# A third value group as seven block products, the rotary table built early, and the log decays stored at once

## The chip, the cores and the metric

The kernel runs on one core of a Trainium2 chip. The metric is the device time of one execution in microseconds (us), lower is better. The kernel before took 2183.36 us (median of three runs, 2181.09 to 2188.8).

## The reference, cut to what matters

One layer of a streaming encoder on a sequence of 1024 tokens with 1024 channels, in float32. The change touches the combined projection and what follows from it directly:

```python
h = rmsnorm(x, ln_pre_mix)
p = h @ w_in
(g_q, g_k, g_v, g_r, g_lr, r_q, r_k, r_v, r_g, a_gla, a_ret) = split(p)
log_a = log_sigmoid(g_lr @ w_gla_decay + b_gla_decay) / GLA_TAU   # log decays of the GLA branch
o_gla = gla_mixer(g_q, g_k, g_v, log_a)                           # gated linear attention, chunks of 64
rq, rk = rope(r_q, positions), rope(r_k, positions)               # cos and sin of positions * inv_freq
o_ret = retention_mixer(rq, rk, r_v)
...
```

Behind it come the output projections of both branches, a mixing projection, and a convolutional feed-forward layer. The change leaves these alone.

## The kernel before

**Numbers and products.** Every float32 matmul is made of three single-pass ones (`product3`, L475 to L477): both operands are split into a high part and a rest (`w_hi`, `w_lo`, `act_hi`, `act_lo`), and high x high, high x rest and rest x high are added up in PSUM. ScalarE or GpSimd makes the high parts, GpSimd or VectorE the rests.

**Queues.** The order of the work on each engine is written out by hand, one function for each engine and stage, with semaphores between them. SyncE's queue (SP) issues nearly all DMAs. SP is in order: behind an instruction that waits, every later DMA waits too.

**The projection stage** runs in this order on TensorE (`proj_pe`):

1. value groups 0 and 1, "plain": each takes 512 columns of values, 8 token tiles by 8 parts of the contraction, so 192 matmuls of 512 columns in two halves of 96;
2. 44 rows of the projection in 22 pairs (`rows_pe`), each pair as seven block products (Strassen's scheme in Winograd's form) of 12 matmuls of 512 columns. The seven use sums of blocks of the activations, `a_sums`, which VectorE and ScalarE make beside value groups 0 and 1 (`rows_sums`, `block_hi`). The last of the seven needs the fourth sum, `S4`;
3. value groups as seven block products (`block_values_pe`), each product 48 matmuls of 256 columns. There are `BLOCK_GROUPS = 2` of them;
4. the small product for the decays' low-rank input (`small_product`, L705 and L706), 32 matmuls;
5. the rest of the value groups, plain. There are six groups in all, so two are left: `EARLY_GROUPS` (call it A) and `EARLY_GROUPS + 1` (B). In the first half of A, `decay_inputs` puts in two times four small matmuls (L718) that give the decays' logits.

**What runs beside A and B.** VectorE and ScalarE turn the logits into log decays (`log_a`, L760 to L805). Then VectorE computes the rotary table in `ang`, `turn` and `rope_out` (a range reduction of 11 steps, L810 to L826, two steps behind the sines), ScalarE takes two sines (L767, L768). GpSimd splits the slabs of B and the first slabs of the next stage (L509, L512). SP stores the values of A, then loads slabs, stores `log_a` (2 MB), stores the table (1 MB), stores more values, waits for both tables to land, and issues the first loads of the next stage (`gla_first_loads`): masks, interval table, two chunks of log decays, keys, queries and values of two tiles, and the gates. The values of B are stored last, and `proj_sp` ends when these stores have landed.

**The GLA stage** begins on TensorE in `first_tile`: `decay(0, 0)` needs the split log decays of the first tile, two pieces of a side projection follow, then `scores(0, 0)`, `decay(0, 1)`, two more pieces, `scores(0, 1)`. ScalarE's order there is `decay(0)`, an eviction, `log_a_hi(2)` (the split of the next chunk of log decays), `decay(1)`. VectorE's `queries(0, 1)` and so `scores(0, 1)` need `decay(1)`. The loads that `log_a_hi(2)` needs are the first DMAs that SP issues in its next phase (`gla_sp`), thus after the last value stores have landed:

```python
            for j in range(RING):
                sp.wait_ge(stored[j], 16 * PROJ_STORES)
```

Of the kernel before, what the change touches and what calls it, by code (L numbers as in the profile page):

```python
# [21 lines left out]
I32 = mybir.dt.int32  # L22
# [8 lines left out]
P = 128  # L31
# [64 lines left out]
RING = 4  # L96
SL_VAL = 0
SL_LR = SL_VAL + 4 * EARLY_GROUPS
BLOCK_GROUPS = 2
# [141 lines left out]
def build(nc, x, positions, w_stream, w_dec, b_dec, ln_post_mix, ln_post_ffn, ln_cols_in, conv_in,  # L241
          ident_in, interval_in, masks_in, ret_dec_in, ret_q_in, ret_k_in, inv_freq_in, eps_in, out):
    ctx = ExitStack()
    with ctx:
# [24 lines left out]
        stat = sb(ctx, "stat", (P, 80))  # L269
        with ExitStack() as s:  # L270
            act_f = [sb(s, f"act_f{i}", (P, KT * SEQ)) for i in range(2)]
# [14 lines left out]
        with ExitStack() as s:  # L286
# [8 lines left out]
            pos_i = sb(s, "pos_i", (P, SEQ), I32)  # L295
            ang = sb(s, "ang", (P, 2, SEQ))
            turn = sb(s, "turn", (P, SEQ))
            rope_out = sb(s, "rope_out", (P, 2, SEQ))
            invf = sb(s, "invf", (P, 1))
# [88 lines left out]
        row_s1 = at(88, "row_s1", (P, 2, HALF))  # L388

# [127 lines left out]
        def norm_sp(sp):  # L517
# [11 lines left out]
            load_slab(sp, 3, 3)  # L529

# [107 lines left out]
        def proj_pe(pe):  # L638
# [82 lines left out]
        def proj_act(act):  # L721
# [44 lines left out]
            act.wait_ge(sem["angle"], ANGLE_STEPS - 2)  # L766
            nc.scalar.activation(rope_out[:, 1, :], ang[:, 0, :], ACT.Sin).then_inc(sem["sin_half"], 1)  # L767
            nc.scalar.activation(ang[:, 1, :], ang[:, 0, :], ACT.Sin, scale=0.5).then_inc(sem["sin_half"], 1)  # L768

            values(EARLY_GROUPS, range(2, 4))  # L770
            values(EARLY_GROUPS + 1, range(2))
            gla_first_parts(act)
            values(EARLY_GROUPS + 1, range(2, 4))

        def proj_dve(dve):
# [25 lines left out]
            for t in range(NT):  # L801
                if t >= 2:
# [7 lines left out]
            nc.vector.tensor_copy(ang[:, 1, :], pos_i[:, :]).then_inc(sem["angle"], 1)  # L810
            dve.wait_ge(sem["angle"], 1)
            nc.vector.tensor_scalar(ang[:, 0, :], ang[:, 1, :], invf[:, 0:1], None, ALU.mult
                                    ).then_inc(sem["angle"], 1)
            dve.wait_ge(sem["angle"], 2)
            magic = 1.5 * 2.0 ** 23
            nc.vector.tensor_scalar(turn[:, :], ang[:, 0, :], 1.0 / (2.0 * math.pi), magic,
                                    ALU.mult, ALU.add).then_inc(sem["angle"], 1)
            dve.wait_ge(sem["angle"], 3)
            nc.vector.tensor_scalar(turn[:, :], turn[:, :], magic, None, ALU.subtract
                                    ).then_inc(sem["angle"], 1)  # L820
            dve.wait_ge(sem["angle"], 4)
            for i, part in enumerate(two_pi_parts()):
                nc.vector.scalar_tensor_tensor(ang[:, 0, :], turn[:, :], -part, ang[:, 0, :],
                                               ALU.mult, ALU.add).then_inc(sem["angle"], 1)
                dve.wait_ge(sem["angle"], i + 5)
            nc.vector.tensor_scalar(ang[:, 0, :], ang[:, 0, :], 3.1415925, -3.1415925,  # L826
                                    ALU.min, ALU.max).then_inc(sem["angle"], 1)
            dve.wait_ge(sem["sin_half"], 2)
            nc.vector.tensor_tensor(ang[:, 0, :], ang[:, 1, :], ang[:, 1, :], ALU.mult
                                    ).then_inc(sem["angle"], 1)  # L830
            dve.wait_ge(sem["angle"], ANGLE_STEPS - 1)
            nc.vector.tensor_scalar(rope_out[:, 0, :], ang[:, 0, :], -2.0, 1.0, ALU.mult, ALU.add
                                    ).then_inc(sem["angle"], 1)

        def proj_sp(sp):
# [17 lines left out]
            value_stores(1, range(4))  # L853
# [31 lines left out]
            block_store(sp, 1, 1)  # L885
            block_store(sp, 1, 0)
            sp.wait_ge(sem["lr_out"], 1)
# [3 lines left out]
            sp.dma_start(pos_i[:, :], positions.to_broadcast((P, SEQ))).then_inc(sem["small_in"], 16)  # L891
            sp.dma_start(invf[:, :], inv_freq_in).then_inc(sem["small_in"], 16)
            for n in range(SL_LR + RING, SL_LR + 2 * RING + 1):
                load(n)
            for g in range(EARLY_GROUPS, N_PLAIN):
                value_stores(g, range(2))
                for n in range(4 * g + 2 * RING + 1, 4 * g + 3 * RING + 1):
                    if n < SL_SIDE + 7:
                        load(n)
                if g == EARLY_GROUPS:  # L900
                    sp.wait_ge(sem["log_a"], NT)
                    sp.dma_start(loga_d.rearrange("t p c -> p t c"), z_sb[:, :, :]).then_inc(sem["tables_stored"], 16)
                    sp.wait_ge(sem["angle"], ANGLE_STEPS)
                    sp.dma_start(rope_d.rearrange("a p n -> p a n"), rope_out[:, :, :]
                                 ).then_inc(sem["tables_stored"], 16)
                value_stores(g, range(2, 4))
                if g == EARLY_GROUPS:
                    sp.wait_ge(sem["tables_stored"], 32)
                    for j in range(RING):
                        sp.wait_ge(stored[j], 16 * (EARLY_GROUPS + ROW_LOADS))  # L910
# [3296 lines left out]
```

## Time and profile before

| what | value |
|---|---|
| median of three runs | 2183.36 us |
| the profiled execution | 2180.39 us |
| its span, first to last instruction | 2178.2 us |
| TensorE busy | 2140.4 us, 98% of the span |
| VectorE, GpSimd, ScalarE busy | 61%, 61%, 36% |
| mean granted TensorE clock | 0.998 |
| mean DMA rate | 144 GB/s |

Matmuls are pipelined, so the time from the start of one to the start of the next tells more than their durations; a stage's length is the difference between two starts. Idle time of an engine other than TensorE costs something only where TensorE waits for it in the end.

### The profile page before, as it was taken

How to read it: one execution, taken by the hardware profiler on the slowest of the kernel's cores; microseconds unless marked ns; L12 is line 12 of the kernel's file. 1: busy time of each engine (PE TensorE's matmuls, PEld its weight loads, DVE VectorE, ACT ScalarE, POOL GpSimd, SP SyncE). 2: the span in 40 equal slices, each digit the busy share in tenths (PEclk: the TensorE clock that was granted, in tenths of full speed). 3: DMA queues.
4: the chain of work that ended last, by engine and by line, in shares of the span. 5: the costliest groups of instructions: out<-in, count | busy, mean ns of one | idle time of the engine just before them, and what ended most of it. 6: DMA issues, size and time to landing. Idle time of an engine off the chain costs nothing. (4 is left out here: it accounts for less than half of the span.)

```text
span 2178.2 us, 28844 instructions
## 1 busy us (share of the span) xinstructions
PE 2140.4 (98%) x10682; PEld 1762.2 (81%) x10682; DVE 1323.6 (61%) x1702; ACT 781.1 (36%) x1275; POOL 1321.8 (61%) x907
## 2 busy tenths in 40 slices
PE   8999999999999999999999999999999999999998
PEld 7888888888988788887776888878778888887887
DVE  7422222222263777768778159854877777779988
ACT  4323333322122222222224134545444444444445
POOL 4787777776554666569875412520799999972000
PEclk9999999999999999999999999999999999999999
DMA  4233333332337344356666755973122332247463
GB/s 178 85 118 107 116 116 117 116 101 94 111 120 247 98 140 141 121 184 179 183 176 212 270 179 150 252 202 133 61 78 88 87 88 87 78 163 251 155 228 134
DMA packets 212729, 312.85 MB, mean 144 GB/s; under 512 B 12464, under 2 KB 129584, under 8 KB 212592
## 3 DMA queue, kind: packets, MB, share of 16 engines
q1 hardware_dynamic: 210272, 306.76, 43.7%
q0 software_dynamic: 2176, 4.19, 1.2%
q8 instruction: 86, 1.41, 0.3%
q14 instruction: 51, 0.42, 0.1%
q10 hardware_dynamic: 144, 0.07, 0.0%
HBM read 220.79 MB, written 90.18 MB: 143 GB/s over the span
## 5 line engine op out<-in xcount | busy, mean ns | idle before, releaser
L475 PE MATMUL psum<-act_hi,w_hi 128*128 128x512 f32 x976 | 389.1, 399 | 3.3 <-POOL w_lo L3802 1.2
L477 PE MATMUL psum<-act_hi,w_lo 128*128 128x512 f32 x976 | 381.0, 390 | 0.0
L476 PE MATMUL psum<-act_lo,w_hi 128*128 128x512 f32 x976 | 380.7, 390 | 0.0
L475 PEld LDWEIGHTS psum<-act_hi,w_hi 128*128 128x128 f32 x976 | 183.3, 188 | 42.9 <-POOL w_lo L3802 2.5
L477 PEld LDWEIGHTS psum<-act_hi,w_lo 128*128 128x128 f32 x976 | 183.2, 188 | 39.5
L475 PE MATMUL psum<-w_hi 128*128 128x512 f32 x532 | 208.4, 392 | 6.3 <-DVE w_lo L3433 5.1
L476 PEld LDWEIGHTS psum<-act_lo,w_hi 128*128 128x128 f32 x976 | 183.5, 188 | 35.7
L477 PE MATMUL psum<-w_hi,w_lo 128*128 128x512 f32 x532 | 207.7, 390 | 0.0
L476 PE MATMUL psum<-w_lo,w_hi 128*128 128x512 f32 x532 | 207.6, 390 | 0.0
L1117 POOL TENSOR_TENSOR w_lo<-w_raw,w_hi 128x512 fp32r<-128x512 f32 x88 | 115.3, 1311 | 70.7 <-ACT w_hi L1075 70.7
L475 PE MATMUL psum<-w_hi,act_hi 128*128 128x512 f32 (+1 forms) x384 | 139.7, 364 | 1.7 <-POOL w_lo L512 1.5
L476 PE MATMUL psum<-w_lo,act_hi 128*128 128x512 f32 (+1 forms) x384 | 139.3, 363 | 0.0
L477 PE MATMUL psum<-w_hi,act_lo 128*128 128x512 f32 (+1 forms) x384 | 139.2, 363 | 0.0
L475 PE MATMUL psum<-a_sums,w_hi 128*128 128x512 f32 x352 | 136.9, 389 | 0.0
L476 PE MATMUL psum<-a_sums,w_hi 128*128 128x512 f32 x352 | 136.9, 389 | 0.0
L477 PE MATMUL psum<-a_sums,w_lo 128*128 128x512 f32 x352 | 136.9, 389 | 0.0
L3802 POOL TENSOR_TENSOR w_lo<-w_raw,w_hi 128x512 fp32r<-128x512 f32 x80 | 125.5, 1578 | 2.8 <-ACT w_hi L3863 2.8
L475 PEld LDWEIGHTS psum<-w_hi 128*128 128x128 f32 x532 | 100.2, 188 | 30.2 <-POOL w_lo L3439 5.0
L477 PEld LDWEIGHTS psum<-w_hi,w_lo 128*128 128x128 f32 x532 | 100.2, 188 | 21.1
L476 PEld LDWEIGHTS psum<-w_lo,w_hi 128*128 128x128 f32 x532 | 100.3, 189 | 20.5
L1117 POOL TENSOR_TENSOR w_lo<-t_sums,w_hi 128x512 fp32r<-128x512 f32 x66 | 85.0, 1289 | 43.3 <-ACT w_hi L1075 43.3
L3863 ACT ACTIVATE w_hi<-u_t 128x512 fp32r<-128x512 f32 x66 | 39.8, 628 | 194.0 <-POOL u_t L3788 120.3
(392 smaller groups left out, 5219.3 us busy)
## 6 DMA issues: line engine op xcount, KB each, us to landing
w_raw<-in_w_stream SPq DMA_DIRECT2D x161, 512.0 KB, 4.3
proj_scratch<-stage SPq DMA_DIRECT2D x44, 512.0 KB, 5.2
r_x<-proj_scratch SPq DMA_DIRECT2D x64, 256.0 KB, 3.7
w_raw<-ffn_scratch SPq DMA_DIRECT2D x55, 256.0 KB, 3.1
value_scratch<-stage SPq DMA_DIRECT2D x24, 512.0 KB, 3.6
w_raw<-in_w_stream SPq DMA_DIRECT2D x44, 256.0 KB, 4.9
ffn_scratch<-u_lin_v SPq DMA_DIRECT2D x22, 512.0 KB, 5.9
w_raw<-ffn_scratch SPq DMA_DIRECT2D x22, 512.0 KB, 4.3
```

The lines of the kernel that those rows point to most:

```text
L475: nc.tensor.matmul(o, s_hi, m_hi, start=start, stop=False)
L476: nc.tensor.matmul(o, s_hi, m_lo, start=False, stop=False)
L477: return nc.tensor.matmul(o, s_lo, m_hi, start=False, stop=stop)
L1117: nc.gpsimd.tensor_tensor(w_lo8[:, n % 8, :], row_block(p, i), w_hi8[:, n % 8, :].bitcast(F32), ALU.subtract).then_inc(sem["u_lo"], 1)
L3802: nc.gpsimd.tensor_tensor(w_lo8[:, n % 8, :], block_raw(p, i), w_hi8[:, n % 8, :].bitcast(F32), ALU.subtract).then_inc(sem["u_lo"], 1)
L3863: nc.scalar.activation(w_hi8[:, n % 8, :], block_raw(p, i), ACT.Copy).then_inc(sem["u_hi"], 1)
```

## The change

One of the two late plain value groups (B) becomes a third block group, so the stage ends with A alone. The rotary table is computed beside value groups 0 and 1, between the sums of activation blocks, in memory that the fourth sum and `row_s1` use later: ScalarE therefore waits for the stored table before it writes the fourth sum's high part. The log decays are stored right behind the first half of A's values. The masks and the interval table are loaded before the wait for the stores, and the loads of the next stage's slabs 4 to 6 stand between and behind the other first loads. The positions and inverse frequencies are loaded at the very start and no longer in front of the decays.

```diff
-BLOCK_GROUPS = 2
+BLOCK_GROUPS = 3
...
@@ norm_sp
             load_slab(sp, 3, 3)
+            sp.dma_start(pos_i[:, :], positions.to_broadcast((P, SEQ))).then_inc(sem["small_in"], 16)
+            sp.dma_start(invf[:, :], inv_freq_in).then_inc(sem["small_in"], 16)
@@ proj_pe
-            for a in range(2):
-                pe.wait_ge(sem["val_evac"], 4 * EARLY_GROUPS + 2 + 2 * a)
-                values(EARLY_GROUPS + 1, a)
@@ proj_act
-            block_hi(8, S4R_HI, S4_F)
             for n in range(6):
                 row_hi(act, n)
+            act.wait_ge(sem["angle"], ANGLE_STEPS - 2)
+            nc.scalar.activation(sines[:, :], ang[:, :], ACT.Sin).then_inc(sem["sin_half"], 1)
+            nc.scalar.activation(turn[:, :], ang[:, :], ACT.Sin, scale=0.5).then_inc(sem["sin_half"], 1)
             values(1, range(2, 4))
             row_hi(act, 6)
             row_hi(act, 7)
+            act.wait_ge(sem["tables_stored"], 32)
+            block_hi(8, S4R_HI, S4_F)
             rows_act(act)
...
             values(EARLY_GROUPS, range(2))
-            act.wait_ge(sem["angle"], ANGLE_STEPS - 2)
-            nc.scalar.activation(rope_out[:, 1, :], ang[:, 0, :], ACT.Sin).then_inc(sem["sin_half"], 1)
-            nc.scalar.activation(ang[:, 1, :], ang[:, 0, :], ACT.Sin, scale=0.5).then_inc(sem["sin_half"], 1)
-
+            gla_first_parts(act)
             values(EARLY_GROUPS, range(2, 4))
-            values(EARLY_GROUPS + 1, range(2))
-            gla_first_parts(act)
-            values(EARLY_GROUPS + 1, range(2, 4))
@@ proj_sp
             value_stores(0, range(2, 4))
-            value_stores(1, range(4))
+            value_stores(1, range(2))
+            sp.wait_ge(sem["angle"], ANGLE_STEPS)
+            sp.wait_ge(sem["sin_half"], 1)
+            sp.dma_start(rope_d[0, :, :], ang[:, :]).then_inc(sem["tables_stored"], 16)
+            sp.dma_start(rope_d[1, :, :], sines[:, :]).then_inc(sem["tables_stored"], 16)
+            value_stores(1, range(2, 4))
...
+            value_stores(EARLY_GROUPS, range(2))
+            sp.wait_ge(sem["log_a"], NT)
+            sp.dma_start(loga_d.rearrange("t p c -> p t c"), z_sb[:, :, :]).then_inc(sem["tables_stored"], 16)
+            gla_table_loads(sp)
+            sp.wait_ge(sem["tables_stored"], 48)
+            for j in range(RING):
+                sp.wait_ge(stored[j], 16 * (EARLY_GROUPS + ROW_LOADS))
+            gla_log_a_load(sp, 0)
+            gla_log_a_load(sp, 1)
+            load(SL_SIDE + 4)
+            gla_first_loads(sp)
+            load(SL_SIDE + 5)
+            load(SL_SIDE + 6)
+            value_stores(EARLY_GROUPS, range(2, 4))
@@ rows_sums (VectorE)
             lo(2, S2_LO, S2_F, S2_HI)
+            angle_turns(dve)
+            angle_reduce(dve, 0, 3)
             lo(3, S3_LO, S3_F, S3_HI)
+            angle_reduce(dve, 3, 7)
+            nc.vector.tensor_scalar(ang[:, :], ang[:, :], 3.1415925, -3.1415925, ALU.min, ALU.max
+                                    ).then_inc(sem["angle"], 1)
+            angle_cosines(dve)
             lo(4, S4_LO, S4_F, S4R_HI)
```

`angle_turns`, `angle_reduce` and `angle_cosines` hold the same steps as L810 to L832 before: four, seven, and the two behind the sines. `gla_table_loads` is the masks' and the interval table's load, taken out of `gla_first_loads`.

## Rows read from the trace of the kernel before

**Rows 1.** The page: busy time of each engine.

```profile
PE 2140.4 (98%) x10682; PEld 1762.2 (81%) x10682; DVE 1323.6 (61%) x1702; ACT 781.1 (36%) x1275; POOL 1321.8 (61%) x907
```

**Rows 2.** Waits of TensorE, whole span: total us, times, longest.

```profile
PE psum L718 <- DVE lr_parts L789: 0.9, 1, 0.9
PE psum L475 <- ACT stage L731: 0.9, 1, 0.9
```

**Rows 3.** Windows: first block group, group B. Busy by engine, clock, DMA share, GB/s.

```profile
524.48:564.80 40.32, 40.32 (x338) 40.31 (x337) 7.95 (x7) 8.33 (x8) 26.20 (x11) 1.00 0.27 96
...
658.90:702.40 43.50, 43.50 (x193) 35.88 (x192) 14.21 (x7) 8.14 (x9) 21.44 (x9) 1.00 0.79 260
```

**Rows 4.** Timeline of TensorE: start us, duration us, then the operation.

```profile
618.89 1.20 PE L718 MATMUL psum<-wd_parts,lr_parts 128*128 128x512 f32 x4 [0.89 <-DVE lr_parts L789]
...
625.40 1.07 PE L718 MATMUL psum<-wd_parts,lr_parts 128*128 128x512 f32 x4
...
702.90 0.47 PE L1855 MATMUL psum<-interval,la_parts 128*128 128x512 f32 x1 [0.27 <-issue]
```

**Rows 5.** Timeline of ScalarE, from the decays' input to the second decay.

```profile
616.77 0.63 ACT L751 ACTIVATE wd_parts<-wd_raw 128x512 fp32r<-128x512 f32 x1 [33.36 <-DMA invf<-in_inv_freq_in]
...
639.96 1.92 ACT L731 ACTIVATE stage<-psum 128x1024 f32<-128x1024 f32 x2
...
711.54 0.63 ACT L1525 ACTIVATE la_parts<-g_la 128x512 fp32r<-128x512 f32 x1 [0.51 <-DMA g_la<-loga_scratch]
712.35 1.14 ACT L1561 ACTIVATE e_t<-psum 128x1152 f32<-128x1152 f32 x1 [0.18 <-PE psum L1859]
```

**Rows 6.** Timeline of SP: start us, then the time until the last of the group was issued.

```profile
610.43 0.42 SPq L890 DMA_DIRECT2D b_all<-in_b_dec  x1
...
703.72 1.29 SPq L839 DMA_DIRECT2D value_scratch<-stage  x2
708.41 1.09 SPq L1460 DMA_DIRECT2D g_la<-loga_scratch  x2
```

**Rows 7.** DMA issues of four stretches (from 607, 666, 681, 700 us): us from issue to landing.

```profile
b_all<-in_b_dec SPq DMA_DIRECT2D x1, 256.0 KB, 3.5
...
loga_scratch<-z_sb SPq DMA_DIRECT2D x1, 2048.0 KB, 9.4
...
g_gate<-proj_scratch SPq DMA_DIRECT2D x1, 512.0 KB, 7.1
value_scratch<-stage SPq DMA_DIRECT2D x1, 512.0 KB, 7.9
...
value_scratch<-stage SPq DMA_DIRECT2D x2, 512.0 KB, 3.4
g_la<-loga_scratch SPq DMA_DIRECT2D x2, 128.0 KB, 2.6
```

**Rows 8.** Windows: the first loads' long part, and the end of them.

```profile
684.00:693.00 9.00, 9.00 (x42) 7.44 (x41) 3.49 (x2) 2.36 (x3) 5.75 (x3) 1.00 1.11 289
693.00:700.00 7.00, 7.00 (x33) 5.79 (x32) 0.00 (x0) 0.00 (x0) 5.76 (x4) 1.00 0.97 359
```

**Rows 9.** Timeline of VectorE: the last log decay and the range reduction.

```profile
640.08 0.69 DVE L798 SCALAR_TENSOR_TENSOR z_sb<-z_sb,z_a 128x512 f32<-128x512 f32 x1 [0.64 <-ACT z_a L763]
...
643.66 21.31 DVE L823 SCALAR_TENSOR_TENSOR ang<-turn,ang 128x1024 f32<-128x1024 f32 x7
```

**Rows 10.** Timelines beside value group 1 and the first rows: VectorE, ScalarE, TensorE.

```profile
87.82 4.49 DVE L1008 TENSOR_TENSOR a_sums<-a_sums_f,a_sums 128x2048 fp32r<-128x2048 f32 x2 [7.21 <-ACT a_sums L735]
...
105.80 1.94 ACT L731 ACTIVATE stage<-psum 128x1024 f32<-128x1024 f32 x2 [4.23 <-PE psum L477]
...
121.92 0.39 PE L475 MATMUL psum<-a_sums,w_hi 128*128 128x512 f32 x1
```

**Rows 11.** Windows near the end of the span, where TensorE waits often.

```profile
1975.00:1980.00 5.00, 2.88 (x12) 2.05 (x11) 5.00 (x4) 2.10 (x4) 5.00 (x4) 0.97 0.14 36
1980.00:1990.00 10.00, 10.00 (x39) 8.13 (x38) 9.86 (x9) 1.79 (x3) 2.62 (x2) 0.85 0.79 255
```

More of the change, by code:

```diff
@@ L269, in build @@
         stat = sb(ctx, "stat", (P, 80))
+        invf = sb(ctx, "invf", (P, 1))
         with ExitStack() as s:
@@ L388, in build @@
         row_s1 = at(88, "row_s1", (P, 2, HALF))
+        turn, ang = at(72, "turn", (P, SEQ)), at(76, "ang", (P, SEQ))
+        pos_i, sines = at(88, "pos_i", (P, SEQ), I32), at(88, "sines", (P, SEQ))
         u_cg = [at(0, "u_cg0", (P, SEQ)), at(4, "u_cg1", (P, SEQ))]
@@ L808, in proj_dve @@
             log_a_tail(NT - 1)
[L810 to L833, printed above, removed]
         def proj_sp(sp):
@@ L890, in proj_sp @@
             sp.dma_start(b_all[:, :], b_dec.to_broadcast((P, GLA_QK))).then_inc(sem["small_in"], 16)
-            sp.dma_start(pos_i[:, :], positions.to_broadcast((P, SEQ))).then_inc(sem["small_in"], 16)
-            sp.dma_start(invf[:, :], inv_freq_in).then_inc(sem["small_in"], 16)
             for n in range(SL_LR + RING, SL_LR + 2 * RING + 1):
                 load(n)
[L895 to L910, printed above, removed]
-                    gla_first_loads(sp)
+            value_stores(EARLY_GROUPS, range(2))
[12 more added lines that the diff above has]
+            value_stores(EARLY_GROUPS, range(2, 4))
             for j in range(RING):
@@ L998, in build, with angle_turns, angle_reduce, angle_cosines @@
         S1_F, S4_F, S2_F, S3_F = [a_sums_f[i] for i in (0, 2, 3, 1)]
+        def angle_turns(dve):
+            dve.wait_ge(sem["small_in"], 32)
+            nc.vector.tensor_copy(ang[:, :], pos_i[:, :]).then_inc(sem["angle"], 1)
+            dve.wait_ge(sem["angle"], 1)
+            nc.vector.tensor_scalar(ang[:, :], ang[:, :], invf[:, 0:1], None, ALU.mult).then_inc(sem["angle"], 1)
+            dve.wait_ge(sem["angle"], 2)
+            magic = 1.5 * 2.0 ** 23
+            nc.vector.tensor_scalar(turn[:, :], ang[:, :], 1.0 / (2.0 * math.pi), magic,
+                                    ALU.mult, ALU.add).then_inc(sem["angle"], 1)
+            dve.wait_ge(sem["angle"], 3)
+            nc.vector.tensor_scalar(turn[:, :], turn[:, :], magic, None, ALU.subtract).then_inc(sem["angle"], 1)
+            dve.wait_ge(sem["angle"], 4)
+        def angle_reduce(dve, lo, hi):
+            for i in range(lo, hi):
+                nc.vector.scalar_tensor_tensor(ang[:, :], turn[:, :], -two_pi_parts()[i], ang[:, :],
+                                               ALU.mult, ALU.add).then_inc(sem["angle"], 1)
+                dve.wait_ge(sem["angle"], i + 5)
+        def angle_cosines(dve):
+            dve.wait_ge(sem["sin_half"], 2)
+            nc.vector.tensor_tensor(ang[:, :], turn[:, :], turn[:, :], ALU.mult).then_inc(sem["angle"], 1)
+            dve.wait_ge(sem["angle"], ANGLE_STEPS - 1)
+            nc.vector.tensor_scalar(ang[:, :], ang[:, :], -2.0, 1.0, ALU.mult, ALU.add).then_inc(sem["angle"], 1)
         def rows_sums(dve):
```

14 lines of the change are left out of this document (6 added, 8 removed).

## The prediction

> **What bounds the kernel now.** I read the page first. TensorE is busy for 98% of the span, and the three other compute engines for 61% or less [rows 1]. So time changes only where TensorE gets fewer or shorter matmuls, or where it waits. Then I read TensorE's waits over the whole span. In the stretch that the change touches they hold two entries of 0.9 us: one for the split input of the decays (L718 behind VectorE's `lr_parts`), one for the last eviction of group B (L475 behind ScalarE's L731) [rows 2]. The reader is to see that no wait of this stretch is large: a gain must come from matmuls, and a loss from waits that aren't there yet. Third, windows give the lengths of the pieces: a block group takes 40.32 us, plain group B 43.5 us, at a full clock, and in the block group the weight loads fill the whole window (40.31 us) [rows 3]. Last come the timelines of the engines and of SP from 600 to 715 us, since group B is also the cover under which the log decays are stored, read back and split, and the first tiles are loaded.
>
> **Term 1: the group.** Plain B is 192 matmuls of 512 columns, 43.5 / 192 = 227 ns each. A block group is 7 x 48 = 336 matmuls of 256 columns, 40.32 / 336 = 120 ns each [rows 3]. The multiplications fall by an eighth (168 against 192 in units of 512 columns), but a 256-column matmul costs more than half of a 512-column one, so the gain is 43.5 - 40.3 = 3.2 us. VectorE (8 us of 40), ScalarE (8) and GpSimd (26) have room in such a window [rows 3], so I expect the third group to run at the pace of the first.
>
> A rule of the Trainium skill speaks of this price: in "TensorE: Matmul & The Clock Gate", section "Back-to-back issue gap", a warm matmul takes N / 2.4 + 2.5 ns, thus 109 ns for 256 columns and 216 ns for 512. By it the term would be 41.4 - 36.7 = 4.7 us instead of 3.2. The rows above show 120 and 227 ns, and weight loads without a gap, so the measurement decides.
>
> **Term 2: the decays' input.** ScalarE's L751 started at 616.77 us, when the load of `invf` had landed [rows 5]. That load and the positions now come at the start of the kernel. The last load in front of L751 is then `b_all`, issued at 610.43 to 610.85 and landed 3.5 us later, at 614.4 [rows 6, 7]. L751 comes 2.4 us earlier relative to the small product, which is more than the 0.9 us that TensorE waits [rows 2, 4]. Gain 0.9 us.
>
> **Term 3: the table beside groups 0 and 1.** Here I must price what the front now has to wait for. VectorE gets 14 more operations of 128x1024 ahead of the fourth sum. A two-input operation of twice that size takes 4.49 / 2 = 2.24 us there, so about 1.1 us each. Beside a busy GpSimd the seven reduction steps took 21.31 / 7 = 3.04 us each [rows 9, 10]. Before, VectorE ended its sums at 87.82 + 4.49 = 92.3 us. It stood idle for 7.2 us before them; four short steps (0.7 us each, an estimate) and three reductions at 1.1 fit in there. Behind the third sum (90.1 us) come four reductions and the clamp: 5.3 us cheap, 15.2 us dear. They end between 95 and 105 us. The sines need ScalarE (about 1.3 us of table load and twice 1.05 us): 102 (it is held by TensorE's pace until then) to 108 us. The cosines add 2 to 4 us, the two stores 3.4 us [rows 7], so the table has landed between 109 and 116 us. Then ScalarE's part of the fourth sum takes 1.9 us, VectorE's 2.24 to 4.4 us: ready between 113 and 122 us. TensorE uses it at 121.92 us [rows 10]. GpSimd is idle or paced by TensorE for half of that time, so I take the cheap side, with 5 us to spare: cost 0. Dear end: 1 us. The evictions of group 1 (L731 at 105.80 us [rows 10]) slip by at most 3 us, and TensorE needs their banks only at the fifth row product, 11 us later. Queued behind ScalarE's new wait are `row_s1` and the high parts of the second pair, needed eight products (22 us) after 105.6 us: covered. At the very start SP issues two more DMAs behind the first slabs: covered too.
>
> **Term 4: what lay under group B.** Everything up to the small product moves by 40.3 us, and the decays' chain by 40.3 - 0.9 = 39.4 us. The GLA stage would start at 702.90 - 3.2 - 0.9 = 698.8 us, if its inputs are there. Now the chain:
>
> - The last log decay was ready at 640.08 + 0.69 = 640.8 us, the first half of A's values evicted at 641.9 us [rows 5, 9]. After: 680.2 and 681.3 us.
> - SP issues both value stores and then the 2 MB store at 681.7 us. It took 9.4 us before [rows 7]. Half a slab's load lay ahead of it then and the table's store (1 MB) came behind it; I take 8.5 us, thus 690.2 us, and 691.1 as the late end, 688.5 as the early one.
> - Four DMAs read two chunks back (2.2 us to issue, 2.6 us to land [rows 6, 7]): 695.0 us. ScalarE and VectorE split the second chunk in 0.6 + 0.7 to 2.9 us (the upper end is what a VectorE operation took beside GpSimd): 696.3 to 698.5 us. TensorE wants it at 698.8 us. No cost, barely; at the late end 0.6 us.
> - All the first loads are now behind that wait. From 691 us on, SP has to move the two chunks (0.5 MB), a slab (0.5), five loads of keys, values and gates (2.6), two slabs (1.05) and the last two value stores (1.05), 5.8 MB in all. The stretch in which such loads ran moved 289 GB/s, the one behind it 359 [rows 8]: 1.05 / 0.359 + 2.6 / 0.289 + 2.1 / 0.359 = 2.9 + 9.0 + 5.8 = 17.7 us. The last store has landed at about 709 us. It can't be earlier than 700.9 + 3.4 = 704.3 us, the issue plus the landing without a backlog [rows 7]; with the 7.9 us of a store behind the gates [rows 7] and two slabs more (2.9 us) it is 711.7 us.
> - Before, the last stores were issued at 703.72 us, `proj_sp` ended with their landing, and `gla_sp` issued the next log decays at 708.41 us. ScalarE was already waiting for them at 711.54 us, and `decay(1)` ran at 712.35 us [rows 5, 6]. ScalarE is in order, so `decay(1)`, VectorE's `queries(0, 1)` and TensorE's `scores(0, 1)` stand behind that load. With SP free at about 709.4 us, `decay(1)` runs 1.0 us later than before. Without this wait it would have run 4.1 us earlier.
>
> So the stall in front of `scores(0, 1)` is about 5 us, and it takes up any shorter wait before it (late `g_la`, late keys for `queries(0, 0)`); they don't add.
>
> **Sum.** -3.2 - 0.9 + 5.1 = +1.0 us on the profiled execution's 2180.39 us (span 2178.2 and 2.2 around it). The median of the runs is 2183.36 us, 3.0 us above; the same change there gives **2184.4 us**. From the bounds: -4.1 with the early end of the stores, +3.3 with the late one, +1 more from the front and +1.5 from the clock (below).
>
> **Rivals.**
>
> 1. *The backlog drains in time* (0.27). The DMAs of the first tiles land fast enough that the last store lands at about 704.3 us. For it: DMA moved 359 GB/s where nothing slow was in the way. Against it: 5.8 MB between 691 and 704 would need 440 GB/s. Part of the way is possible: between -4.1 and -1 us, 2179.3 to 2182.4 us.
> 2. *The log decays come back late, and the clock falls* (0.10). The one mechanism is the 2 MB store: each us that it lands later delays first tile and last store alike. From 5.5 us more than I take (14 us instead of 8.5) the loss passes 6.5 us, 2190 us or more. Near the end of the span, where TensorE worked 2.88 of 5 us, the granted clock went from 1.00 to 0.85 over 10 us, that is, to 1.2 GHz for a part of it [rows 11], which costs 1.5 us. A stall of 5 us or more could do that here. The Trainium skill, "TensorE: Matmul & The Clock Gate", section "What's actually happening", has the same rule: the clock is halved when the engine was idle. By it rival 2 and my forecast would be up to 1.5 us longer.
> 3. *The front binds* (0.05). The fourth sum comes behind 121.92 us because the reduction runs at 3.04 us a step throughout: +1 to +4 us on top, 2185 to 2189 us.
> 4. *The group is cheaper than the row says* (0.03), at the page's 109 ns per matmul: the third group and the two others would have to differ. 336 x 0.011 = 3.7 us more, 2181 us.
> 5. Something that I don't see, either way (0.03). My own case has 0.52.
>
> **Numbers.** About 0.3% (6.5 us) is what a measurement of this kernel can tell from no change. Nearly all cases lie within it; the ends count through the scatter of runs (2181 to 2189 us). Faster 0.11, same 0.76, slower 0.13. The range reaches from the drained backlog less 1.3 us of scatter to rival 2's beginning: 2178 to 2190 us.
>
> **What would show it.** Right: three windows of 40.3 us for the block groups; no wait at L718; the table's stores landed before 116 us and no TensorE wait near 122 us; GLA's first L1855 at about 699 us; a wait of some 5 us of TensorE in front of the second L1873 group; ScalarE's L1525 for the third chunk waiting on DMA `g_la`; SP's first L1460 of the next phase at about 709 us. Wrong: if that L1460 is at 704 to 705 us, rival 1 holds; if L1855 itself starts behind 702 us, the store of the log decays was later than I took; if the clock falls under 1.00 at 710 us, its cost is on top.

## The result, and the profile after

The changed kernel took 2195.2 us (median of 18 runs, 2184.49 to 2200.82), the kernel before 2183.83 us beside it (18 runs, 2179.55 to 2189.14). The ratio is 1.0047 with an interval of 1.0035 to 1.0058: slower, by 0.5%, more than the scatter of the runs explains, and 5 us beyond the end of my range. The profiled execution of the changed kernel took 2194.13 us (span 2192.3).

TensorE's waits over the whole span of the changed kernel (total us, times, longest), to be read against [rows 2]:

```profile
PE psum L1882 <- DVE k_lev L1734: 7.5, 3, 6.0
...
PE psum L473 <- POOL w_lo L2576: 5.0, 2, 4.1
...
PE psum L715 <- DVE lr_parts L784: 1.8, 1, 1.8
```

The first is the stall in front of `scores(0, 1)` that Term 4 describes. The second is in the y stage, 600 us later, where the diff changes nothing. The third is the split input of the decays, 0.9 us in [rows 2].

Windows of the three block groups, of the first tile, and of the y stage (us; busy time of TensorE, its weight loads, VectorE, ScalarE, GpSimd; clock; DMA share; GB/s):

```profile
524.90:565.30 40.40, 40.40 (x339) 40.40 (x338) 8.02 (x8) 8.39 (x9) 26.22 (x11) 1.00 0.27 93
565.30:605.60 40.30, 40.30 (x338) 40.30 (x337) 8.46 (x8) 8.31 (x9) 26.26 (x11) 1.00 0.32 106
605.60:645.60 40.00, 40.00 (x336) 40.00 (x334) 8.43 (x7) 5.11 (x5) 14.40 (x12) 1.00 0.30 106
...
709.00:716.00 7.00, 6.99 (x48) 5.53 (x44) 1.02 (x3) 0.19 (x1) 0.00 (x0) 1.00 0.55 204
716.00:724.00 8.00, 2.03 (x31) 1.92 (x31) 4.42 (x7) 2.77 (x4) 4.19 (x4) 0.66 0.40 125
718.51:721.97 3.46, 0.00 (x1) 0.00 (x1) 2.57 (x5) 1.35 (x2) 2.14 (x2) 0.50 0.20 48
721.97:725.34 3.37, 3.37 (x35) 3.06 (x36) 2.67 (x5) 0.63 (x1) 3.29 (x4) 0.50 0.33 106
...
1330.00:1340.00 10.00, 5.88 (x26) 4.59 (x25) 7.96 (x12) 4.96 (x8) 10.00 (x2) 0.99 0.56 158
```

The third group runs at the pace of the first. From 716 us on TensorE has 2.03 us of work in 8, and the granted clock falls to 0.50 (1.2 GHz) for 6.8 us, from 718.51 to 725.34 us. The wait lasts until 721.97 us, so half of this stretch lies in the wait and costs nothing. In the other half, 3.4 us, TensorE works at half speed: that costs 1.7 us on top of the wait.

SP from the log decays' store to the third chunk's load (start us, us until issued), to be read against [rows 6]:

```profile
682.68 1.29 SPq L809 DMA_DIRECT2D value_scratch<-stage  x2
684.02 0.49 SPq L874 DMA_DIRECT2D loga_scratch<-z_sb  x1
...
693.84 1.15 SPq L1468 DMA_DIRECT2D g_la<-loga_scratch  x2
...
698.55 2.58 SPq L1455 DMA_DIRECT2D g_v<-value_scratch  x1
701.17 0.47 SPq L1448 DMA_DIRECT2D g_gate<-proj_scratch  x1
701.69 2.67 SPq L489 DMA_DIRECT2D w_raw<-in_w_stream  x2
704.40 0.94 SPq L809 DMA_DIRECT2D value_scratch<-stage  x2
714.52 1.09 SPq L1468 DMA_DIRECT2D g_la<-loga_scratch  x2
```

ScalarE and TensorE behind it, against [rows 5] and [rows 4]:

```profile
656.36 0.63 ACT L752 ACTIVATE wd_parts<-wd_raw 128x512 fp32r<-128x512 f32 x1 [32.46 <-DMA b_all<-in_b_dec]
...
717.72 0.63 ACT L1534 ACTIVATE la_parts<-g_la 128x512 fp32r<-128x512 f32 x1 [8.53 <-DMA g_la<-loga_scratch]
718.26 1.11 ACT L1570 ACTIVATE e_t<-psum 128x1152 f32<-128x1152 f32 x1
```

```profile
701.18 0.47 PE L1864 MATMUL psum<-interval,la_parts 128*128 128x512 f32 x1 [0.38 <-DVE la_parts L1670]
...
721.97 1.55 PE L1882 MATMUL psum<-q_lev,k_lev 128*64 128x64 f32 x24 [5.98 <-DVE k_lev L1734]
```

The reader should see one chain: the last value stores are issued at 704.40 us, the next load waits for their landing until 714.52 us, ScalarE waits 8.53 us for that load, `decay(1)` runs at 718.26 us instead of 712.35, and TensorE stands 5.98 us.

DMA landings of the stretch 700 to 706 us, against [rows 7]. The last value stores took 8.6 us to land behind the gates and the slabs, 3.4 us before:

```profile
w_raw<-in_w_stream SPq DMA_DIRECT2D x2, 512.0 KB, 7.3
value_scratch<-stage SPq DMA_DIRECT2D x2, 512.0 KB, 8.6
```

### Where the time lies, in many traces

One trace was not enough here. The table sets the start of the same TensorE matmul in a run against its start in the first trace of the kernel before (us later; the columns are times in that trace). The column 60 stands ahead of all work that the edits move, apart from two small loads.

```
trace                 60    740    921   1300   1345   1500    end
before, 2nd        -0.2   -0.1   -0.5    2.0    2.0    4.7    4.7
before, 3rd         2.0    2.1    2.0    1.6    1.6    4.6    4.8
changed, 1st        0.2    5.7    5.9    7.4   13.5   13.9   14.0
changed, 2nd        0.1    6.0    5.6    7.0    7.0    7.7    7.7
changed, 3rd        0.6    6.1    6.0    5.4   11.3   16.0   16.1
changed, 4th        2.2    8.2    7.8    9.1    9.1   14.9   15.2
group_only          0.0   24.3   24.6   23.7   23.7   26.3   26.5
table_early         0.1   -0.8    0.8    3.0    3.0    2.7    2.6
stores_first        1.6    5.8    5.0    4.4    4.4   10.1   10.2
keep_busy           0.1    4.2    3.1    4.4    7.2   13.8   13.9
backlog_more        0.2    8.0    7.2    6.6    6.6    5.7    5.9
bias_apart          1.7    4.8    4.9    4.5    4.5    7.4    7.4
chunks_first        2.0   -2.5   -3.2   -2.2   -2.2   -1.6   -1.4
before_shift        1.9    7.7    6.8    5.7    5.7   10.1    9.9
after_y             0.2    7.6    7.6    8.8   16.6   19.3   19.4
after_y19           2.1    8.1    7.4    8.9    8.9   12.3   12.3
chunks_y19          2.0   -2.5   -2.8   -1.7   -1.7    0.7    0.8
before_y            1.8    2.0    1.9    4.1    4.1    2.6    2.7
chunks_y            0.4   -4.0   -4.3   -4.8   -4.8   -2.4   -2.4
```

Four places move. The start of the kernel, ahead of 60 us, differs by up to 2.4 us from execution to execution, in both kernels (mean 0.8 and 0.6): the traces that are 1.6 us or more late at 60 us have 3.4 us of half clock near 15 us, the others none. To read the effect of an edit on the first tile, take the column 60 off. The first tile is in every trace of the changed kernel: 5.5 to 6.0 us with the start taken off (mean 5.7) against 0.0 to 0.1 in the kernel before. The y stage (1300 to 1345) costs 6 us in two of the four and nothing in the others: in the first trace 4.1 us of a wait, and 1.7 us for the half clock behind it. The mix stage (1469 us) costs 0 to 3 us in the kernel before and 0.4 to 5.8 in the changed one (mean 1.9 and 2.9). So 0.1 + 5.7 + 3.0 + 1.0 and 0.2 in between make 10 us of the medians' 11.4.

### The profile page after: what moved, and what is told of

It reads as the page before. It is cut to its first block and busy times, and to the rows that moved or that the text cites. A ratio compares the mean times of both kernels' runs of the same rounds, so it can differ in the third digit from the quotient of the medians.

```text
span 2192.3 us, 29169 instructions
## 1 busy us (share of the span) xinstructions
PE 2142.1 (98%) x10826; PEld 1768.6 (81%) x10826; DVE 1323.8 (60%) x1709; ACT 786.0 (36%) x1279; POOL 1335.2 (61%) x910
## 3 DMA queue, kind: packets, MB, share of 16 engines
q0 software_dynamic: 2176, 4.19, 1.2%
## 5 line engine op out<-in xcount | busy, mean ns | idle before, releaser
L473 PE MATMUL psum<-w_hi,act_hi 128*128 128x512 f32 (+1 forms) x368 | 128.4, 349 | 1.9 <-POOL w_lo L510 1.6
L474 PE MATMUL psum<-w_lo,act_hi 128*128 128x512 f32 (+1 forms) x368 | 127.9, 348 | 0.0
L475 PE MATMUL psum<-w_hi,act_lo 128*128 128x512 f32 (+1 forms) x368 | 127.9, 348 | 0.0
L1125 POOL TENSOR_TENSOR w_lo<-t_sums,w_hi 128x512 fp32r<-128x512 f32 x66 | 87.3, 1323 | 39.4 <-ACT w_hi L1083 39.4
```

Of the source, the lines that this page charges most:

```text
L473: nc.tensor.matmul(o, s_hi, m_hi, start=start, stop=False)
L474: nc.tensor.matmul(o, s_hi, m_lo, start=False, stop=False)
L475: return nc.tensor.matmul(o, s_lo, m_hi, start=False, stop=stop)
L1125: nc.gpsimd.tensor_tensor(w_lo8[:, n % 8, :], row_block(p, i), w_hi8[:, n % 8, :].bitcast(F32), ALU.subtract).then_inc(sem["u_lo"], 1)
```

## The experiments

**group_only and table_early**: the two halves of the change, each alone.

```diff
 group_only: the kernel before with
-BLOCK_GROUPS = 2
+BLOCK_GROUPS = 3
-            for a in range(2):
-                values(EARLY_GROUPS + 1, a)
 table_early: the changed kernel with BLOCK_GROUPS = 2 and group B plain and last
```

> Only the third block group: the rotary table stays behind the log decays, and the stores and loads of the stage's end stay in their old order, now under group A alone. Nothing is left out. Late-store theory: the 2 MB store waits behind the loads of slabs that follow GpSimd's pace (about 705 us instead of 684), then come 9 us of store and 3 us of loads, so the GLA stage begins near 722 us instead of 701, and the time is 15 to 25 us above the kernel before. If the cover of the stores did not matter, it would be 3 us below.

> Only the early rotary table and the early store of the log decays, with two block groups and group B plain again. Nothing is left out. Late-store theory: group B covers the stores and first loads again, so there is no long wait in the first tile; within 2 us of the kernel before, 0 to 1 us better if the wait at the decays' input shrinks. Rival (the front costs something that the trace of one execution doesn't show, such as slower sums of activation blocks): 3 us or more above the kernel before, with a TensorE wait near 122 us. Rival (the y stage suffers from any shift of the stages before it): a wait in the y stage here too.

group_only: 2206.73 us, 23.7 over the kernel before, and one wait of TensorE of 24.5 us at the GLA stage's first matmul, with a half clock of 23.9 us. That is inside the forecast. table_early: 2185.47 us, ratio 1.0014 (1.0004 to 1.0024), and no wait of 1 us in the first tile. The median is 2.4 us over the kernel before, a little more than the 2 us that I allowed for. The third group brings the loss with it, since it takes away the cover of group B: under a plain group B the last stores land in time. The early table and the early store of the log decays bring that loss down, from 24 us to 11.

**stores_first**: are the loads ahead of the last value stores what costs?

```diff
             gla_log_a_load(sp, 1)
-            load(SL_SIDE + 4)
-            gla_first_loads(sp)
-            load(SL_SIDE + 5)
-            load(SL_SIDE + 6)
+            gla_tile_loads(sp, 0)
             value_stores(EARLY_GROUPS, range(2, 4))
+            gla_log_a_load(sp, 2)
...
 def gla_sp
+            gla_tile_loads(sp, 1)
+            gla_gates(sp, 0)
+            for n in range(SL_SIDE + 4, SL_SIDE + 7):
+                stream_load(sp, n)
             for t in range(NT):
```

> The changed kernel, with the late half of A's value stores issued right behind the first tile's loads, the third chunk of log decays loaded behind them while SP is still in the projection stage, and the second tile's loads, the gates and slabs 4 to 6 moved behind the end of proj_sp. Nothing is left out of the computation. Late-store theory (the loss is the wait for the landing of the last value stores, which stand behind about 5 MB of first loads, and the fall of the clock in the hole that it makes): the 6.0 us wait in front of the second scores group is under 1.5 us, decay(1) runs at 708 to 711 us instead of 718.3, the clock stays at 1.00 there, and the time is 8 to 10 us below the changed kernel, 1 to 4 us below the kernel before if the later stages behave as before. Rival (the 4.1 us wait of TensorE in the y stage, which the changed kernel has and the kernel before has not, follows from the change itself): that wait stays, and the time is 2 to 6 us above the kernel before.

It took 2191.09 us (1.0029, 1.0014 to 1.0044), still 8 us over the kernel before, where I expected 1 to 4 us under it. The wait of the third chunk was gone, but the fourth chunk's load now stood behind the second tile, gates and slabs, and landed late in its turn. At 740 us its trace is 4.2 us late with the start taken off, against 5.7. Of these, 1.6 us come from a half clock at 663 us, behind Term 2's wait. The tile itself still cost 4.6 us of 7.7: the loss had shrunk and moved. SP, ScalarE and TensorE's waits from 700 to 760 us:

```profile
714.16 2.13 SPq L1466 DMA_DIRECT2D g_la<-loga_scratch  x2
```

```profile
723.58 0.63 ACT L1536 ACTIVATE la_parts<-g_la 128x512 fp32r<-128x512 f32 x1 [3.97 <-DMA g_la<-loga_scratch]
```

```profile
PE psum L1884 <- DVE k_lev L1736: 4.7, 2, 4.1
```

**backlog_more**: a dose the other way. `spare_d` is a scratch of 1 MB.

```diff
             load(SL_SIDE + 6)
+            sp.dma_start(spare_d[:, :, :], stage[:, 0:2, :]).then_inc(sem["tables_stored"], 16)
             value_stores(EARLY_GROUPS, range(2, 4))
+            sp.wait_ge(sem["tables_stored"], 64)
```

> The changed kernel with one more 1 MB store (half of the first A values once more, to a scratch) ahead of the last value stores. It adds 1.05 MB / 0.359 = 2.9 us to the backlog that SP waits for. Theory (the landing of the last value stores sets the first tile's wait): SP issues the third chunk 2.9 to 3.5 us later than 714.5 us, decay(1) runs at 721 to 722 us instead of 718.3, TensorE's wait before scores(0, 1) is 9 us instead of 6, and the half-clock stretch is as long or longer by 3.4 us; time 2.9 to 4.6 us over the changed kernel. Rival (something else sets it): SP's issue and the wait stay within 1 us.

The third chunk was issued at 716.77 us (+2.3), `decay(1)` ran at 720.62 (+2.4), TensorE waited 8.34 us (+2.4). That is the slope the theory asks for, a little under the 2.9 us of the sum. The half clock began in the wait again, at 720.8 us, and TensorE had 3.3 us of it behind the wait: no more than in the changed kernel, where I had expected a longer one. The median, 2194.42 us (10 runs, 11.1 us over the kernel before beside it), is not above the changed kernel's, so the 2.9 to 4.6 us that I forecast for the time did not show; the scatter of later stages covers 2 us.

```profile
716.77 1.09 SPq L1471 DMA_DIRECT2D g_la<-loga_scratch  x2
```

```profile
724.33 1.55 PE L1885 MATMUL psum<-q_lev,k_lev 128*64 128x64 f32 x24 [8.34 <-DVE k_lev L1737]
```

**bias_apart**: the decays' input (Term 2). The later waits on the two counts are moved with it.

```diff
-            sp.dma_start(b_all ...).then_inc(sem["small_in"], 16)
+            sp.dma_start(b_all ...).then_inc(sem["tables_stored"], 16)
-            act.wait_ge(sem["small_in"], 16 * 7)      # ahead of the copy of wd_raw
+            act.wait_ge(sem["small_in"], 16 * 6)
+            dve.wait_ge(sem["tables_stored"], 48)     # ahead of the additions of b_all
...
```

> The changed kernel, but the decays' bias b_all has a semaphore of its own: ScalarE's L752 waits for the four small weight loads alone, VectorE's additions for the bias. In the changed kernel L752 started at 656.36 us, 5.2 us after b_all was issued, VectorE's L778 then took 2.44 us, and TensorE waited 1.76 us at L715. Theory (the bias load is what is late): L752 at 653 to 655 us, the wait at L715 0 to 0.2 us, everything up to the log decays' store 1.7 us earlier, and the first tile gains between 0 and 1.7 us more. Time 1 to 4 us under the changed kernel's 2195.2, with the first tile's wait still 4 us or longer. Rival (VectorE's step beside GpSimd is what is late): the wait at L715 stays at 1 us or more.

L752 ran at 654.04 us and TensorE had no wait between 600 and 690 us. The GLA stage began at 700.25 us instead of 701.18, in a trace that was 1.5 us later at 60 us: the edit is worth 2.4 us there. The first tile's wait stayed at 6.0 us. Its median was 2188.35 us (1.0024, 1.0013 to 1.0035), 5.1 us over the kernel before, lower than 2.4 us explain; its trace had no loss in the y stage.

**keep_busy**: does the clock's fall come from the wait, and what does it cost? In `scores(0, 1)`, ahead of its wait:

```diff
+                if e == 1:
+                    pe.wait_ge(sem["g_mask"], 1)
+                    for _ in range(26):
+                        nc.tensor.matmul(psum[:, S_BANK, :], act_hi[:, 0:P], act_hi[:, 0:HALF], start=True, stop=True)
```

> The changed kernel, with 26 matmuls of 128x512 whose result is overwritten put in before scores(0, 1), in the place where TensorE waits 6.0 us: 26 x 0.227 = 5.9 us of work. They add work and take none away. Theory (the clock fell because of that wait, and gave 3.4 us away): no half clock between 700 and 740 us, the wait before L1883 under 0.7 us, and the time from the first GLA matmul to 740 us is 3 to 3.5 us shorter than in the changed kernel (which lost 3.4 us at half clock there). Time about 3 us under the changed kernel run beside it. Rival (the clock falls for another reason): the half clock stays, and the time is equal or longer by up to 1 us.

The window from 716 us has TensorE full, at full clock:

```profile
716.00:724.00 8.00, 8.00 (x62) 6.54 (x61) 4.83 (x8) 3.05 (x5) 4.48 (x5) 1.00 0.35 115
```

So the fall follows from the wait: fill the wait with work that does nothing, and the clock stays. With the start taken off, this trace is 4.1 us late at 740 us, where the changed kernel's four are 5.5 to 6.0 (mean 5.7): 1.6 us given back. That is what 3.4 us at half speed behind the wait cost in the first trace (1.7 us); in the four traces they were 3.4 to 5.9 us, thus 1.7 to 2.9. I had expected 3 to 3.5 us, because I had counted the whole 6.8 us, with the part that lies in the wait. At 921 us the difference is 2.5 us (3.1 against 5.6), but 740 us is nearer to the edit, and between the two the traces move for other reasons: 0.8 to 0.9 us in stores_first, backlog_more and before_shift, too. The median, 2193.48 us (8 runs), shows no more than 2 us of it: this trace lost 2.8 us in the y stage, where GpSimd's step before the usual one took 9.8 us, and 6.6 in the mix stage.

**chunks_first**: each load by when it is wanted. On top of stores_first and bias_apart:

```diff
 def gla_sp
             gla_tile_loads(sp, 1)
-            gla_gates(sp, 0)
-            for n in range(SL_SIDE + 4, SL_SIDE + 7):
-                stream_load(sp, n)
             for t in range(NT):
...
                     gla_log_a_load(sp, 2 * t + 3)
+                if t == 0:
+                    stream_load(sp, SL_SIDE + 4)
+                    gla_gates(sp, 0)
+                    stream_load(sp, SL_SIDE + 5)
+                    stream_load(sp, SL_SIDE + 6)
```

> The kernel with the value stores first, and on top: the fourth chunk of log decays is loaded ahead of slabs 4 to 6 and the gates (before, it came behind them, landed 7 us after its issue and TensorE waited 4.1 us), and the bias has its own semaphore. Theory (each stall of the first tile is a load late behind a backlog, not a lack of DMA rate): ScalarE's parts of the third and fourth chunk have no DMA wait, TensorE has no wait over 1.5 us between 700 and 740 us and a full clock there; the offset against the kernel before is -4.0 us at 668 us and still -2 to -4 us at 760 us. The retention and later stages keep their +1 to +6 us, so 2180 to 2187 us. Rival (the DMA rate binds the first tiles whatever the order): another load takes over, TensorE waits 3 us or more before 760 us, 2188 us or more.

2177.96 us beside 2183.28, ratio 0.9978 (0.9965 to 0.9991): faster than both kernels. SP and TensorE from 700 to 724 us:

```profile
701.26 1.27 SPq L810 DMA_DIRECT2D value_scratch<-stage  x2
702.58 1.77 SPq L1467 DMA_DIRECT2D g_la<-loga_scratch  x2
...
710.53 1.92 SPq L1467 DMA_DIRECT2D g_la<-loga_scratch  x2
```

```profile
709.00:716.00 7.00, 7.00 (x52) 5.67 (x54) 4.95 (x8) 1.82 (x4) 4.43 (x4) 1.00 0.70 233
716.00:724.00 8.00, 7.24 (x70) 5.87 (x65) 5.88 (x11) 2.77 (x3) 4.86 (x4) 1.00 0.64 220
```

The same bytes move, and no wait of the tile exceeds 0.8 us. With the start taken off, the trace is 4.4 us ahead of the kernel before at the GLA stage's first matmul and 4.5 us at 740 us: the 4.1 us of Terms 1 and 2 are all there.

**More traces, and before_shift.** The kernel before and the changed kernel were traced again (the table above), and 26 such matmuls went into the kernel before, where nothing waited.

> The kernel before once more, for its trace. In one profile of the changed kernel TensorE lost 5.7 us in the y stage (1327 to 1330 us), in another nothing; two kernels of this study lost 4 us in the mix stage at 1470 us. If such losses come and go in the kernel before too, this trace or the next has one of 2 us or more behind 740 us that the first does not have; if they belong to the changed kernel, both traces agree with the first within 1.5 us from 740 us to the end.

> The changed kernel once more. The first tile's wait (6.0 us) and a half clock of 6.8 us near 720 us as in the two traces so far, so +5.5 to +7 us against the kernel before at 740 us. In the y and mix stages: a loss of 2 us or more if such losses are what lifts its median 11 us over the kernel before; none if the one at 1327 us was an accident.

> The kernel before with the same 26 matmuls of 128x512 (5.9 us) put in before scores(0, 1), where it had no wait of 1 us or more: it starts the rest of the layer 5 to 5.9 us later, at a full clock and with nothing else changed. Theory (the losses in later stages do not depend on how late those stages start): the median is 5 to 6.5 us over the kernel before. Rival (a later start by itself brings the losses of the y and mix stages): 9 to 12 us over it, as the changed kernel was.

The kernel before loses 3 us in the mix stage in two of three traces, and before_shift's trace 4.4, so a loss there belongs to both; in the changed kernel and its edits it reached 5.8 and 6.6 us, and why it is larger there is open. The y stage's loss appeared only in the changed kernel and in two edits of it (keep_busy, after_y). before_shift took 2190.31 us beside 2183.94 (+6.4): a late start alone brings its own length and nothing more; the rival falls.

**after_y, before_y, chunks_y, after_y19, chunks_y19**: the y stage. GpSimd makes every third low part there. In the changed kernel's first trace one of them, step 19, took 11.35 us beside a VectorE that had no gap from 1323 to 1338 us, and the next, step 22, 1.3 us; alone one takes 1.3. The step ended at 1339.08 us, 1.1 us after VectorE's run did. In the traces without the loss step 19 took 1.3 to 1.6 us and step 22 5.1 to 5.8, which cost no wait. The first row is the changed kernel, the second the kernel before (its step 22):

```profile
1327.73 11.35 POOL L2576 TENSOR_TENSOR w_lo<-act_f,w_hi 128x512 fp32r<-128x512 f32 x1 [5.03 <-ACT w_hi L2571]
```

```profile
1328.48 5.14 POOL L2567 TENSOR_TENSOR w_lo<-act_f,w_hi 128x512 fp32r<-128x512 f32 x1 [6.59 <-ACT w_hi L2562]
```

```diff
-        POOL_Y_LOWS = range(1, RET_STEPS, 3)
+        POOL_Y_LOWS = [s for s in range(1, RET_STEPS, 3) if s not in (19, 22)]   # after_y: (22, 25)
```

> The changed kernel with two of the 19 y-stage steps that GpSimd makes (22 and 25, the ones that ran 12.6 us together at 1327.73 us) given to VectorE, 0.6 us each there. Theory (GpSimd's step stretched beside a VectorE without gaps is what costs 6 us in two of three executions): no loss at 1319 to 1345 us in its trace, and a median 3 to 6 us under the changed kernel's, that is 5 to 8 us over the kernel before. Rival 1 (the loss goes to the neighbouring steps 19 or 28): a wait of 2 us or more there. Rival 2 (the y stage is not where the median went): the median stays 10 to 12 us over.

> The kernel before with the same edit of the y stage. None of its three traces lost time there, so the time stays within 1.5 us of the kernel before; a gain of 3 us or more would say that its untraced executions have that loss as well.

> The changed kernel with the y-stage steps 19 and 22 taken from GpSimd and given to VectorE (after_y had taken 22 and 25, one too late). Three of five traces with the changed kernel's front lost 6 to 8 us at step 19, so that loss is worth some 3.5 us in the mean. Theory: no GpSimd step over 6 us between 1310 and 1345 us, no TensorE wait there, and a median 3 to 5 us under the changed kernel's, 6 to 8 us over the kernel before. Rival 1: the loss goes to step 16 or 25, a wait of 2 us or more there. Rival 2: the median stays at 10 to 12 us over.

> The kernel with the chunks first and the bias apart, with steps 19 and 22 given to VectorE. None of its two traces lost time in the y stage, so the edit can only take a loss away that its other executions have: 2176 to 2181 us, 3 to 7 us under the kernel before, and no wait between 700 and 740 us over 1 us.

I read the row of the two steps as 22 and 25 at first, one too late. after_y took steps 22 and 25; step 19 was still there and stretched to 12 us, TensorE waited 4.7 us, and the time stayed at 2194.46 us, 10.5 over the kernel before:

```profile
1329.16 11.95 POOL L2576 TENSOR_TENSOR w_lo<-act_f,w_hi 128x512 fp32r<-128x512 f32 x1 [5.04 <-ACT w_hi L2571]
```

after_y19 took 19 and 22. GpSimd's next step there came only at 1345.57 us, with its usual 1.29 us:

```profile
1321.09 3.13 POOL L2576 TENSOR_TENSOR w_lo<-act_f,w_hi 128x512 fp32r<-128x512 f32 x1 [6.87 <-ACT w_hi L2571]
1345.57 1.29 POOL L2576 TENSOR_TENSOR w_lo<-y,w_hi 128x512 fp32r<-128x512 f32 x1 [21.35 <-ACT w_hi L2571]
```

The one trace says little, since two of the changed kernel's four had no loss either; the runs say more. The median was 2189.04 us beside 2184.52, ratio 1.0024 (1.0014 to 1.0035), and none of 12 runs was over 2192.5, where 13 of the changed kernel's 18 were. after_y, the same edit on the wrong steps, shows that it is step 19 that counts. So the y stage carries some 6 us of the median (6.9 against the changed kernel, 5.9 against after_y, each against the kernel before beside it; 3.0 in the mean of four traces), and the 4.5 us that are left answer to the first tile's 5.7. before_y took 2181.83 beside 2184.00, 0.9993 (0.9984 to 1.0002). It had steps 22 and 25 taken, not 19, so it can't tell whether the kernel before has the loss; that it has not rests on its three traces and on those of before_y, before_shift, table_early and group_only, none of which has it. chunks_y19: 2178.53 beside 2184.52, 0.9977 (0.9967 to 0.9986), the same as chunks_first. chunks_y (22 and 25): 2180.99 beside 2184.00, 0.9993 (0.9980 to 1.0006), over the 2176 to 2180 that I expected; 4 of its 12 runs are above 2186, none of chunks_y19's above 2181.2. A loss at step 19 in some of its executions would fit that; no trace shows one.

## Why the prediction was wrong

- **Term 1** held. Windows of 40.3, 40.3 and 40.0 us against group B's 43.5; together with Term 2, chunks_first and bias_apart are 4.4 us ahead at the GLA stage's first matmul, where I had forecast 4.1. The rule of the Trainium skill that Term 1 sets beside its rows ("TensorE: Matmul & The Clock Gate", section "Back-to-back issue gap") is given there for a single isolated matmul, not for a stream with a weight load for each. So its 4.7 us was no price for this group; the rows' 120 ns held.
- **Term 2** had the wrong sign. I took the landing of `b_all` as 3.5 us [rows 7]; from 651.13 us it took 5.2. VectorE's next step then ran 2.44 us beside GpSimd, and TensorE waited 1.8 us: +0.9 instead of -0.9. bias_apart shows that the bias was what held it. In 3 of the 10 traces with that wait (stores_first, after_y, group_only) the clock fell behind it too, for 3.4 us.
- **Term 3** held: cost 0, and no wait of TensorE between 60 and 520 us. The four late reductions took 9.0 us, about in the middle between my cheap and my dear price for them; the fourth sum's high part began at 111.09 us when the table had landed, its rest at 113.04:

```profile
90.79 9.01 DVE L991 SCALAR_TENSOR_TENSOR ang<-turn,ang 128x1024 f32<-128x1024 f32 x4
...
113.04 2.79 DVE L1010 TENSOR_TENSOR a_sums<-a_sums_f,a_sums 128x2048 fp32r<-128x2048 f32 x1 [6.00 <-ACT a_sums L732]
```

- **Term 4** is the step that failed, by size and not by mechanism. Forecast: stores landed and SP free at 709.4 us (691 and the 17.7 of the sum give 708.7; the rest has no reason there), `decay(1)` at 713.4. Measured: 714.5 and 718.3. The 5.1 us are: the log decays' store issued at 684.0 instead of 681.7 (2.3: the value stores ahead of it went out 1.0 later, behind Term 2, and SP took the 1.3 us to issue them that I had counted as nothing); its landing 9.8 us instead of 8.5 (1.3; of these 3.6 us my start of the backlog at 691 held 0.8); and the backlog 20.7 us from there (693.84 to 714.52) instead of the 18.4 that I left for it (2.3). I had made the sum of MB over rates, and it wanted SP's own time too: SP was still issuing slabs until 704.4 us, since each issue behind a full queue took up to 2.6 us.
- **The clock** was told as a possibility of 1.5 us and left out of the sum. It fell in every trace of the changed kernel and cost 1.7 us in the first (1.7 to 2.9 in the four); keep_busy gave 1.6 back. The size was right, leaving it out was not. With the start taken off, the changed kernel is 2.0 us ahead in front of the first tile and 5.5 us late behind it. Of these 7.5 us the wait is 6.0, the clock 1.7; the 0.2 that they are too much I can't place.
- **Added up**, the first tile came out 4.7 us worse than my +1.0 (mean 5.7): the GLA stage began 2.1 us later than I had it against the kernel before (-2.0 for -4.1), the wait was 0.9 us longer than the 5.1 of the sum, the clock came to 1.7. That alone is about 2189 us, as after_y19 shows (2189.04), and lies inside my range. What put the median outside is the y stage.
- **Rival 2** ("the log decays come back late, and the clock falls") named this outcome, with 0.10 and a trigger of 5.5 us in the 2 MB store's landing. Only 1.3 us came from there; the rest came from issue times and the queue. Its chance should have been the largest, because the bounds of three terms pointed the same way and each one fed the same load.
- **The y stage** was in no case of mine: the sum had no term for it, only the 0.03 of rival 5. It carries some 6 of the 11.4 us. That one GpSimd step there, step 19, is stretched, and that giving it to VectorE takes the time away, is shown. Why it happens with the changed kernel's front is not. In the traces with the third group and the early table whose y stage is as it was (also those without the loss) VectorE ran 0.4 to 0.5 us later against TensorE from 1316 us on than in the first trace of before; keep_busy is the exception, 1.1 us at 1313 us and 0.1 behind it. In the other two traces of before, before_shift, table_early and group_only the difference was 0.0. VectorE's first wait for a slab of that stage was 3.09 us in the changed kernel and 2.52 before. What makes that load later stays open.

## What to carry to other kernels

When a wait for the last stores stands in front of the next stage's first loads, put the loads in the order in which they are wanted and the stores ahead of every load that can come later; the bytes are the same, and here the order (with the bias apart) took the median from 11 us over the kernel before to 5 us under it. Of these 16 us about 10 stand at the first tile; the rest is the y stage's loss, which the traces with the new order don't have, and why is open. Price a backlog by the issue times of the queue as well as by MB over GB/s. Add the clock's fall to a new TensorE wait of the size seen here, but count only the half clock behind the end of the wait: 1.5 to 2.9 us, whether the wait was 4 us or 24. Take several traces before you explain a median: here the first one of the kernel before was 4.7 and 4.8 us shorter than the two others, and one of the changed kernel could have hidden the y stage. And compare traces from a point ahead of the edit: the start alone moved them by up to 2.4 us.

## What the runs showed of the hardware

- A wait of TensorE of 6.0 us came with 6.8 us at 1.2 GHz, so in 8 of 8 traces with a wait of 6.0 to 8.3 us at that place; one of 24.5 us came with 23.9 us at it; the waits of 0.8 us in chunks_first's first tile with none. The half clock began 1.0 to 3.6 us before the end of those 8 waits, and 20.5 us before the end of the long one. So TensorE worked at half speed for 3.3 to 5.9 us behind the 8, and for 3.4 us behind the long one. All 8 waits of 4.1 to 4.7 us, one in stores_first's first tile and seven in later stages, had it too. At the retention stage's start a wait of 3.0 us was followed by 3.4 us at it in the changed kernel's first trace, and one of 2.8 us by none in the kernel before's. Filled with idle matmuls, the same 5.9 us left the clock at 1.00.
- A GpSimd operation on 128x512 took 1.3 us alone, and 5 to 12 us beside a VectorE that ran two-input float32 operations without a gap. Whether it ends before TensorE needs it, 7.3 us after its start for step 19, changes from execution to execution. The Trainium skill, "SBUF — State Buffer", section "SBUF: two separate sides", says that a VectorE operation with two inputs in SBUF and a GpSimd operation that reads SBUF exclude each other for a whole instruction, whichever starts first. The traces fit with that: in the changed kernel's second trace step 19 took 1.34 us and VectorE's 0.68 us operation beside it 1.77. In the first trace the same step took 11.35 us, while 14 VectorE operations ran back to back at their usual length, and ended 1.1 us after the last of them; read by that rule, it lost to each of them in turn.
- A 512 KB store landed in 3.1 us at 682.7 us, with no slab or tile load ahead of it, and in 8.6 us at 704.4 us behind values, gates and slabs, and SP needed up to 2.6 us to issue one DMA there, 0.5 us otherwise.
